# The last column group of two attention projections goes by half units beside the first heads

## What is computed

```python
for i in range(DEPTH_2):
    mod = silu_c @ ada_w[i] + ada_b[i]
    sh1, sc1, g1, sh2, sc2, g2 = [m[:, None, :] for m in jnp.split(mod, 6, axis=-1)]
    h = rms_norm(x, norm_mix_g[i]) * (1.0 + sc1) + sh1
    if i % N_MIXERS == 0:
        y = diff_attention(h, a_w_qkv[j], ...)      # 8 heads, two maps of 64 each, values 128 wide
    else:
        y = chunked_attention(h, b_w_qkv[j], ...)   # 16 heads of 64
    x = x + g1 * y
    h = rms_norm(x, norm_ffn_g[i]) * (1.0 + sc2) + sh2
    x = x + g2 * grouped_moe(h, ...)
```

## Time and profile before

| | |
|---|---|
| median of 3 runs | 1216.38 us (1215.29 to 1219.71) |
| profiled execution, its own time | 1217.9 us |
| its span on the core | 1216.1 us |
| mean granted TensorE clock | 0.98 |
| PE busy | 1106.9 us, 91% of the span |
| DVE busy | 593.3 us, 49% |
| ACT busy | 432.2 us, 36% |
| DMA | 356.14 MB, mean 293 GB/s |
| HBM read | 351.89 MB |

### The profile page before, as it was taken

The page is one execution under the profiler, slowest core; times in us unless marked ns, Lnnn a source line. Parts: engine busy times, 40 slices in busy tenths (PEclk is TensorE's granted clock), DMA queues, the critical chain, the costliest instruction groups (busy, mean ns, idle before and its releaser), DMA issues.

```text
span 1216.1 us, 17412 instructions
## 1 busy us (share of the span) xinstructions
PE 1106.9 (91%) x6792; PEld 742.0 (61%) x6792; DVE 593.3 (49%) x1175; ACT 432.2 (36%) x738; POOL 94.5 (8%) x189
## 2 busy tenths in 40 slices
PE   6999787989999999988999999887999999999986
PEld 6878444779999977855744343325887754343422
DVE  3588352566666656747513322226765532232223
ACT  6445321464445555536412010104546441020100
POOL 0201232320000000022000000002000000000000
PEclk9999989999999999998999999999999999999998
DMA  9956699698777744693679999997675479999995
GB/s 300 259 189 210 216 350 368 186 368 249 212 231 229 226 130 173 220 356 142 273 285 409 409 409 409 408 409 246 226 280 222 149 282 410 409 408 410 409 409 225
DMA packets 164174, 356.14 MB, mean 293 GB/s; under 512 B 10616, under 2 KB 79480, under 8 KB 163968
## 3 DMA queue, kind: packets, MB, share of 16 engines
q1 hardware_dynamic: 147056, 295.81, 66.8%
q0 software_dynamic: 17024, 59.26, 13.9%
q10 hardware_dynamic: 16, 0.02, 0.0%
HBM read 351.89 MB, written 7.36 MB: 295 GB/s over the span
## 4 chain that ended last, share of the span: by engine, by line
PE 69%; DMA 16%; DVE 9%; ACT 4%; issue 2%; POOL 0%; SPq 0%; ACTq 0%; DVEq 0%; POOLq 0%
PE bank L572 36%; PE bank L1124 12%; PE bank L1134 8%; DMA ering<-in_ada_w 4%; DMA ering<-in_moe_w_up 3%; DMA work<-in_moe_w_up 3%; DMA a_raw<-in_moe_w_up 3%; PE bank L1093 3%; PE bank L517 2%; DVE wlo L562 2%; DMA work<-in_ada_w 1%; DMA wraw<-in_w_up 1%; PE bank L731 1%; ACT whi L556 1%; PE bank L844 1%
## 5 line engine op out<-in xcount | busy, mean ns | idle before, releaser
L562 DVE TENSOR_TENSOR wlo<-wraw,whi 128x1024 fp32r<-128x1024 f32 x150 | 179.3, 1221 | 63.5 <-ACT whi L556 62.2
L556 ACT ACTIVATE whi<-wraw 128x1024 fp32r<-128x1024 f32 x150 | 153.8, 1054 | 53.2 <-PE bank L572 41.6
L572 PE MATMUL bank<-a_hi,whi 128*128 128x256 f32 x512 | 147.7, 289 | 1.3 <-DVE a_lo L761 1.1
L572 PE MATMUL bank<-a_lo,whi 128*128 128x256 f32 x512 | 146.2, 285 | 0.0
L572 PE MATMUL bank<-a_hi,wlo 128*128 128x256 f32 x512 | 146.1, 285 | 0.0
L1124 PE MATMUL bank<-ering,work 128*64 128x512 f32 x576 | 129.6, 595 | 9.9 <-DMA ering<-in_moe_w_up 5.6
L1324 DVE TENSOR_TENSOR work<-work,bank 128x512 f32<-128x512 f32 x16 | 11.0, 687 | 204.6 <-PE bank L1124 204.6
L572 PE MATMUL bank<-whi,a_hi 128*128 128x512 f32 x256 | 101.6, 397 | 5.8 <-DVE a_lo L761 3.0
L572 PEld LDWEIGHTS bank<-a_hi,whi 128*128 128x128 f32 x512 | 99.5, 194 | 8.4 <-issue 6.4
L1232 ACT ACTIVATE o_hi<-work 128x512 fp32r<-128x512 f32 x32 | 20.2, 631 | 236.8 <-DVE work L1292 236.3
L572 PE MATMUL bank<-whi,a_lo 128*128 128x512 f32 x256 | 99.9, 390 | 0.0
(11 more groups left out here) (324 smaller groups left out, 1856.8 us busy)
## 6 DMA issues: line engine op xcount, KB each, us to landing
ering<-in_moe_w_up SPq DMA_DIRECT2D x36, 1024.0 KB, 18.4
ering<-in_moe_w_down SPq DMA_DIRECT2D x36, 1024.0 KB, 18.1
ering<-in_moe_w_gate SPq DMA_DIRECT2D x36, 1024.0 KB, 17.4
ering<-in_ada_w POOLq DMA_DIRECT2D x52, 512.0 KB, 5.8
wraw<-in_w_in SPq DMA_DIRECT2D x28, 512.0 KB, 7.3
wraw<-in_a_w_qkv SPq DMA_DIRECT2D x24, 512.0 KB, 4.5
work<-in_moe_w_down SPq DMA_DIRECT2D x12, 1024.0 KB, 18.9
work<-in_moe_w_gate SPq DMA_DIRECT2D x12, 1024.0 KB, 15.8
```

What stands on the lines that cost most here:

```text
L556: nc.scalar.activation(w_hi(c), wraw[:, c % RING, :], ACT.Copy).then_inc(w_hi_done, 1)
L562: nc.vector.tensor_tensor(w_lo(u[0]), wraw[:, u[0] % RING, :], w_hi(u[0]).bitcast(F32), ALU.subtract).then_inc(w_lo_done, 1)
L572: mm = nc.tensor.matmul(out_ap, l, r, start=first and n == 0, stop=last and n == len(terms) - 1)
```

## The change

PE makes only five column groups in the loop. Of the sixth it makes two half units ahead of the first scores, and the other six between the steps of the attention, by the table `LAST_HALVES`. For that banks 2 and 3 stay with the projection: scores of the first heads all use banks 0 and 1 (in layer 1 head 1 uses 5 and 6), by the table `SCORE_BANKS`, and wait for DVE's reading of the scores just before them. ACT's two copies of the sixth group stand between the exponentials of step 4 and the copy of head 3. The bundles 40 to 47 go by the table `ADA_HEADS`, and their pieces lie elsewhere; POOL no longer waits for the whole projection ahead of the pieces 42 and 43.

```diff
-ADA_TAIL = [0, 1, 2, 0, 1, 2, 11, 12, 13, 16, 14, 15, 13, 14, 15, 13]
+ADA_TAIL = [0, 1, 2, 0, 1, 2, 11, 12, 13, 16, 13, 13, 14, 15, 13, 14]
+LAST_HALVES = [[4, 6, 7, 8] + [8] * 8, [4, 6, 7, 8] + [8] * 16]
+ADA_HEADS = [41, 42, 43, 43, 44, 45, 46, 47, 48, 48]
...
-        def unit_columns(pe, u, part, banks, turn=None):
+        def unit_columns(pe, u, part, banks, turn=None, halves=(0, 1)):
-            wait_lo(pe, u)
-            chunk_ready(pe, turn, 2 * part)
-            for kk in range(2):
+            if 0 in halves:
+                wait_lo(pe, u)
+                chunk_ready(pe, turn, 2 * part)
+            for kk in halves:
...
-            mm.then_inc(w_used, 1)
+            if 1 in halves:
+                mm.then_inc(w_used, 1)
...
+        SCORE_BANKS = {1: [(0, 1), (5, 6)] + [(0, 1)] * 4 + [(2, 3), (0, 1)],
+                       2: [(0, 1)] * 4 + [(2, 3), (0, 1), (2, 3), (0, 1)]}
...
             def scores(*ns_):
-                for n in ns_:
-                    if n >= nb * maps:
-                        pe.wait_ge(sc_read, m0 + n + 1 - nb * maps)
+                if ph == 0:
+                    if ns_[0] >= nb:
+                        pe.wait_ge(sc_read, ns_[0] + 1 - nb)
+                else:
+                    g = ns_[0] // 2
+                    if scores_before(ph, g) is not None:
+                        pe.wait_ge(sc_read, m0 + 2 * scores_before(ph, g) + 2)
+                    elif SCORE_BANKS[ph][g] == (2, 3):
+                        pe.wait_ge(qk_evac, 12 * ph)
...
                 scores(0, 1)
+                if ph == 1:
+                    scores(2, 3)
+                last(-1)
             for i in range(units + 2):
...
-                if ph == 1 and i + 1 < units:
-                    scores(2 * i + 2, 2 * i + 3)
-                if ph == 2 and i % 2 == 0 and i + 2 < units:
+                if ph == 2 and i % 2 == 0 and i + 2 < units and not single(i // 2 + 1):
                     scores(i + 2, i + 3)
...
                 if after is not None:
                     after(i)
+                if ph == 1 and i + 2 < units:
+                    scores(2 * i + 4, 2 * i + 5)
+                if ph == 2 and i % 2 == 0 and i + 2 < units and single(i // 2 + 1):
+                    scores(i + 2, i + 3)
+                if last is not None:
+                    last(i)
...
-            pool.wait_ge(w_used, U_WO[0])
             for n in range(ADA_FFN + 2, ADA_FFN + 6):
+                if n == ADA_FFN + 4:
+                    pool.wait_ge(w_used, U_WO[0])
                 load_ada(pool, n)
...
-                if ADA_FFN + 6 + n < ADA_N:
-                    load_ada(pool, ADA_FFN + 6 + n)
+                if 1 <= n <= 2:
+                    load_ada(pool, ADA_FFN + 5 + n)
...
+                halves = [0]
+                def last_units(to):
+                    for n in range(halves[0], to):
+                        unit_columns(pe, (U_QKV[l] + 20 + n // 2, None, 0), n // 2, psum[2:4], None, (n % 2,))
+                    halves[0] = max(halves[0], to)
...
-                for cg in range(6):
+                for cg in range(5):
...
+                pe.wait_ge(qk_evac, 12 * l + 8)
+                last_units(2)
                 pe.wait_ge(qkt_done, 16 * (l + 1))
-                pe.wait_ge(qk_evac, 12 * (l + 1))
-                attention_pe(pe, 1 + l, None, (lambda i: ada(min(ADA_FFN + 1 + i, ADA_N))) if l == 0 else None)
+                pe.wait_ge(qk_evac, 12 * l + 10)
+                attention_pe(pe, 1 + l, None, (lambda i: ada(ADA_HEADS[i])) if l == 0 else None,
+                             lambda i: last_units(min(LAST_HALVES[l][i + 1], 8)))
...
+                def between(i):
+                    if i == 4:
+                        evacuated(5)
+                    if l == 0 and i == A_H:
+                        acol_copy(3)
```

More of the change, by code:

```diff
@@ L803, in att_depth, with scores_before @@
             return 2 if ph == 0 else 4 // ATT[ph][1], (2, 3, 4)[ph]
+        SCORE_BANKS = {1: [(0, 1), (5, 6)] + [(0, 1)] * 4 + [(2, 3), (0, 1)],
+                       2: [(0, 1)] * 4 + [(2, 3), (0, 1), (2, 3), (0, 1)]}
         def score_bank(ph, i, m):
-            return psum[2 + i % 2] if ph == 0 else psum[ATT[ph][1] * (i % att_depth(ph)[0]) + m]
+            if ph == 0:
+                return psum[2 + i % 2]
+            n = ATT[ph][1] * i + m
+            return psum[SCORE_BANKS[ph][n // 2][n % 2]]
+        def scores_before(ph, g):
+            return max((f for f in range(g) if SCORE_BANKS[ph][f] == SCORE_BANKS[ph][g]), default=None)
         def value_bank(ph, n):
@@ L824, in att_value, with attention_pe @@
             return (lambda t: v_one[:, t, n, :]), 65
-        def attention_pe(pe, ph, before=None, after=None):
+        def attention_pe(pe, ph, before=None, after=None, last=None):
             units, maps = ATT[ph]
@@ L846, in scores, with single @@
                             mm.then_inc(sc_ps, 1)
+            def single(g):
+                return scores_before(ph, g) == g - 1
             if ph == 0:
@@ L2168, in _, with evacuated @@
                     acol_copy(2)
-                for cg in range(6):
-                    for j in range(4):
-                        splits(min(U_QKV[l] + 4 * cg + j + 1 + AHEAD, U_WO[l]))
+                def evacuated(cg):
                     act.wait_ge(w_used, U_QKV[l] + 4 * cg + 4)
@@ L2186, in _ @@
                         nc.scalar.activation(dst, src, ACT.Copy).then_inc(qk_evac, 1)
+                for cg in range(5):
+                    for j in range(4):
+                        splits(min(U_QKV[l] + 4 * cg + j + 1 + AHEAD, U_WO[l]))
+                    evacuated(cg)
+                    g = 4 * l + cg
                     if cg < 4:
@@ L2202, in squares @@
                     ins.then_inc(os_done, 1)
-                attention_act(act, 1 + l, (lambda i: acol_copy(3) if i == A_H else None) if l == 0 else None)
+                def between(i):
[3 more added lines that the diff above has]
+                        acol_copy(3)
+                attention_act(act, 1 + l, between)
                 splits(U_WO[l] + 2)
```

## The result

The changed kernel takes 1222.19 us (median; 1219.17 to 1225.67) against 1216.63 us (1215.29 to 1219.71) for the kernel before in the same measurement: ratio 1.0039, 95% interval 1.0025 to 1.0054. I had forecast 1215.2 us, between 1207.5 and 1219.0. Its profiled execution took 1219.17 us, with a span of 1217.4 us, against 1217.9 and 1216.1 us before.

The account below looks back on a forecast made before the run. PE was taken as 69% of the chain and DMA 16%, with layer 1's attention hanging on pieces. Layer 1 +1.0 and layer 2 -2.2 made -1.2 us: 1216.4 to 1215.2 us, range 1207.5 to 1219.0.

Parts of the forecast that it names:

- Layer 2: Layer 2's attention: idle time covered by moved matmuls, less small costs, -2.2 us, between -1.1 and -2.5.
- Both waits: Start of layer 2's attention: PE's waits for ACT's copy (1.27 us) and first exponentials (1.19 us) go, 2.46 us.
- that rival: Layer 2: ACT's copies and narrower banks give back 1.1 and 0.8 us, kernel at 1216.8 us; chance 0.10.
- Layer 1, PE's side: Layer 1, engines alone: 126th unit used at about 537.0 us, bundle 47 at about 552.5 against 559.42, 6.9 us earlier.
- this slower rival: Layer 1: piece 42 comes late and shifts the 126th unit and loads; costs 4.8 us, 1220.0 us; chance 0.13.
- The tail: Layer 1 after bundle 47: 6.7 us to ACT's square root instead of 7.46, as a 0.77 us wait goes.
- Layer 1, the bytes: Layer 1: 9.2 MB at 409 GB/s takes 22.5 us; bundle 47 at about 561.2 us, 1.8 us later than before.
- The clock: Layer 1: granted clock adds nothing, being 0.80 where PE waited between steps, and PE waits there again.
- The Trainium skill's rule: Layer 1 DMA: SP's and POOL's transfers interleave on the same 16 engines, so pieces and experts' weights are one stream.
- layer 1's term: Whole of layer 1's attention: +1.0 us, square root at 567.9 us against 566.88.
- -0.6 to +1.1: Layer 1 bytes: spread of the likeliest case for a stream between 390 and 420 GB/s, 23.6 to 21.9 us.
- the signs that I had named for a wrong forecast: Bundle 47 before 558 us, PE waiting at bundle 42, or PE in layer 2 waiting for ACT behind step 4.

Follow-up runs that it names:

- run 48: Not a follow-up run or kernel: the words are "In a run 48 matmuls", meaning 48 matmuls in one uninterrupted sequence, 11.02 us in layer 2.
- held changed kernel: Changed kernel with SP's experts' loads 7 to 10 of layer 1 issued only once bundle 45 is used: 1212.44 us, ratio 0.9955 to the kernel before.
- the scores first and the hold: Changed kernel, but layer 1 runs six half units together after the first scores, old piece places, experts' loads 7 to 10 held: 1209.49 us, ratio 0.9933.
- two runs, held: Changed kernel, layer 1's six half units as two then four behind bundle 40, old piece places, experts' loads 7 to 10 held: ratio 0.9956.
- two runs, not held: Changed kernel, layer 1's six half units as two at once and four behind bundle 40, old piece places, experts' loads not held: ratio 1.0026.
- the third: Changed kernel measured once more, unaltered, beside the kernel before: ratio 1.0020, stages 55.9 and 39.3 us.
- held old order: Kernel before, with only SP's experts' loads 7 to 10 of layer 1 held back by one wait: ratio 0.9975, layer 1 48.9 us.
- other two profiles: Profiles of the two unaltered repeats of the changed kernel beside the kernel before: ratios 1.0044 and 1.0020.
- the control: Changed kernel's text with its new tables and functions, but both layers in the old order, against the kernel before: ratio 1.0011.

## Why the prediction was wrong, step by step

The forecast was -1.2 us, and the first measurement 4.7 us by its ratio. Of the 5.9 us between them layer 1's stage has 2.3, layer 2's 0.5, and 3.1 us lie in neither and stay open.

**Layer 2** (forecast -2.2, measured -1.7 us): mechanism right, size 0.5 us off. Both waits, 2.46 us, are gone, and the only new one ahead of the last head is 0.19 us for DVE. What I had not costed is that half units run slower between small products. In a run 48 matmuls take 11.02 us in layer 2; in the changed chain the first pieces read

```profile
912.09 2.84 PE bank L576 x12
914.93 0.86 PE bank L868 x8
915.78 2.95 PE bank L576 x12
918.73 0.86 PE bank L868 x8
919.59 2.96 PE bank L576 x12
```

where a quarter of 11.02 us is 2.76 us: each of these stretches costs 0.1 to 0.2 us more. ACT's copies in the middle cost nothing that shows, so that rival fell.

**Layer 1, PE's side** was right. Counted from the last key turn I had put the last half unit's end at 537.0 - 516.1 = 20.9 us, and it came at 541.11 - 519.80 = 21.3 us. Piece 42 was no wait: this slower rival fell too. The tail was right as well: 6.7 us from bundle 47 to the square root, forecast; the timeline of ACT has, beside the bundle's start at 567.27 us,

```profile
573.85 0.29 ACT L643 ACTIVATE sm<-sm 128x16 f32<-128x16 f32 x1
```

which is 6.6 us.

**Layer 1, the bytes: the step that failed.** Mechanism right, term too small. I had "9.2 MB, at 409 GB/s 22.5 us", and with it bundle 47 at 24.2 us behind the release; it came at 567.27 - 541.11 = 26.2 us. The bytes were right: 380 GB/s over 16 us and 360 over 9 us are 9.3 MB. The rate was not. 409 GB/s is what the engines did in the best 16 us of before. From the release of the loads to the landing of piece 47 (the same columns as above) the kernel before did 359 on the average, and the changed kernel 357:

```profile
528.00:557.40 29.40, 23.60 (x169) 13.05 (x168) 21.06 (x111) 17.88 (x70) 12.06 (x24) 0.88 0.93 359
541.00:567.20 26.20, 16.40 (x111) 9.61 (x109) 14.66 (x58) 10.40 (x39) 12.75 (x26) 0.80 0.93 357
```

In the changed kernel the 16 us in the middle (547 to 563 us) have 412 GB/s, but the first 6 us only 325, and the last 4, with nothing but POOL's pieces left, 188. Piece 47 is not in a stream, but in a chain (piece 44, bundle 44, piece 47) that is as long as its parts: 2.3 + 0.5 + 10.6 + 2.0 + 0.3 + 0.6 + 9.8 = 26.1 us. It was lost early: bundle 44 was to start 10 us behind the release and started 13.4 us behind it. I could have seen this beforehand: the same sum made for the kernel before gives 528.1 + 25.7 + 1.1 = 554.9 us for piece 47, and the earlier trace rows have it landed at 551.9 + 5.5 = 557.4 us. I tested the model on nothing, and it was already 2.5 us short where the answer was known, with no experts' load left beside piece 47, which was late because bundle 44 had to make room for it. The 2.0 us between 24.2 and 26.2 are nearly all of the 2.3 us by which layer 1 was missed (+3.3 instead of +1.0).

**The clock** was "no term of its own". In the course of the wait of 6.65 us PE fell to the lower level (0.50 from 551 to 559 us; bundle 44 took 1.94 us where the others take 1.06), so room for piece 47 came 0.9 us later. The held changed kernel (518 to 557 us) and the one with the scores first and the hold had full clock over the whole stretch; of the latter:

```profile
518.00:555.00 37.00, 34.19 (x238) 20.95 (x236) 24.89 (x121) 21.38 (x77) 14.84 (x30) 1.00 0.87 329
```

So this wait cost 0.9 us more than its own length; behind the waits of 1.64 us (held changed kernel) and 2.27 us (two runs, held) the bundle took its usual 1.06 us, and behind one of 2.14 us (two runs, not held) 1.93 us, so the length of the wait alone does not tell.

**The Trainium skill's rule** ("DMA: Bandwidth & Descriptors", section "Issuing engines are not separate DMA queues") was borne out: holding back SP's four loads, and nothing on POOL, shortened the stage that waits for POOL's pieces by 3.8 and 8.3 us.

**The range and the chances.** The right sign of layer 1's term was in the text, its size outside of my "-0.6 to +1.1" for the stream. The measured stages, +3.3 and -1.7, would have put the time at 1218.0 us, still inside the range. The first measurement stands above that by the part that stays open; the third, by its ratio (1218.8 us), would have been inside. None of the signs that I had named for a wrong forecast came: bundle 47 was not early, PE did not wait at bundle 42, nor for ACT in the middle of layer 2. I had named no sign for a stream that is slower than its best stretch.

**What the change is worth.** Its idea has three parts, and they have different signs. The scores ahead of the last six half units are worth 4.1 us in layer 1 (48.9 to 44.8 us, both held; 3.1 us of it are the waits of 1.27 and 1.80 us, and some of the rest is clock, since bundle 41 took 1.93 us in the held old order); in layer 2, with half units between the steps too, it is 1.7 us. The half units between the steps of layer 1, with the places of the pieces that go with them, cost 2.9 us. The release of experts' loads and pieces 9 us later costs the other 4.5 us (8.3 - 3.8): it is only to be seen when nothing holds the loads. Scores first, no half units between the steps of layer 1, and the loads held make 0.9933: by the ratio 8.2 us faster than before.

## What to carry to other kernels

When work is moved behind other work, look at what its last instruction releases, on every queue, and at what starts at the same moment as that: here a half unit that PE could do at any time was what two queues waited for. Make the sum of bytes over time first for the kernel that you have, where the landing is known, and carry over the rate that comes out of it, with the gaps; and where a load waits for the use of an earlier one, add up the chain rather than the stream. A transfer that nothing needs soon is best issued behind the ones that something waits for: one wait on SP was worth 3.8 us in the old order and 8.3 us in the new one, where the reordering of three engines alone lost time.

## What the runs showed of the hardware

- Between a release on POOL and its next DMA there can stand 2.30 us in which it waits for nothing that the profile shows (541.11 to 543.41 us). It stands in the changed kernel's other two profiles at the same place. In the kernel before it stands ahead of piece 44 too (531.99 to 534.29 us), while piece 42 there went 0.3 us after its release (528.1 to 528.40 us). In each case of 2.30 us POOL had issued two or four DMAs in the few us before, and at the 0.3 us it had stood idle for 19.60 us; whether that is the cause no run shows.
- PE's clock may be granted at the lower level for a short stretch in one profile and not in another, with the same instructions ahead of it: 1.6 us in layer 2 of the control, and as much in layer 2 of the kernel with the scores first and the hold. A stage of 40 us can thus differ by 4% between two single profiles; it takes a second one to read a change of that size.
- In 14 profiles of these kernels the last key turn of layer 1, ahead of which nothing was changed, stood between 515.79 and 521.55 us. A landmark behind the common part has to be the zero.
